# A decoder layer's attention stage: nine threshold searches dealt gap by gap, and the sixteen query blocks in another order

## The reference

```python
s = jnp.einsum('bqhd,bsd->bqhs', iqb, ikf)                       # 8 index heads of 64
idx_score = jnp.einsum('bqhs,bqh->bqs', jax.nn.relu(s), iwb * w_scale)
idx_score = jnp.where(causal[None], idx_score, NEG_INF)
_, sel = lax.top_k(idx_score, n_sel)                             # n_sel = 256
...
logits = jnp.where(valid[:, :, None, None, :], logits, NEG_INF)
p = jax.nn.softmax(logits, axis=-1)
```

## Time and profile before

| | us |
|---|---|
| median of 3 runs | 4710.19 |
| lowest and highest | 4708.51, 4710.79 |
| the profiled execution | 4710.05 |
| its span in the trace | 4708.1 |
| attention in it, first logits to the end of the last block's values | 613.8 to 1898.7 |

### The profile page before, as it was taken

The page is one execution under the profiler, slowest core; times in us unless marked ns, Lnnn a source line. Parts: engine busy times, 40 slices in busy tenths (PEclk is TensorE's granted clock), DMA queues, the critical chain, the costliest instruction groups (busy, mean ns, idle before and its releaser), DMA issues. The chain is left out here.

```text
span 4708.1 us, 69036 instructions
## 1 busy us (share of the span) xinstructions
PE 4350.5 (92%) x24163; PEld 3164.7 (67%) x24163; DVE 3098.5 (66%) x4884; ACT 1816.1 (39%) x2677; POOL 933.7 (20%) x1126
## 2 busy tenths in 40 slices
PE   8999978899988887399999999999999999999987
PEld 4444434444444443299998988989899998998961
DVE  2567747887778885245555655657566776776767
ACT  1222233343433333133334444444444555555530
POOL 0000012121111112211111212212122222222235
PEclk9999989999999998699999999999999999999996
DMA  5444230011010000344445536455466566666668
GB/s 187 119 121 123 66 93 24 21 25 19 15 28 15 15 13 14 97 148 165 156 136 208 191 138 228 170 200 201 174 224 217 208 231 229 213 232 225 217 219 335
DMA packets 525084, 666.35 MB, mean 142 GB/s; under 512 B 59201, under 2 KB 389441, under 8 KB 524897
## 3 DMA queue, kind: packets, MB, share of 16 engines
q1 hardware_dynamic: 400368, 484.87, 31.1%
q10 hardware_dynamic: 97984, 93.93, 6.1%
q0 software_dynamic: 26576, 85.56, 4.7%
HBM read 543.93 MB, written 120.36 MB: 141 GB/s over the span
## 5 line engine op out<-in xcount | busy, mean ns | idle before, releaser
L1956 DVE TENSOR_TENSOR w_lo<-w_raw,w_hi 128x2048 fp32r<-128x2048 f32 x386 | 874.5, 2286 | 557.7 <-ACT w_hi L2040 557.7
L1864 PE MATMUL gu<-x_hi,w_hi 128*128 128x240 f32 (+8 forms) x4096 | 1196.1, 292 | 21.5 <-DVE up L1971 15.7
L1867 PE MATMUL gu<-x_lo,w_hi 128*128 128x240 f32 (+8 forms) x4096 | 1192.6, 291 | 0.0
L1868 PE MATMUL gu<-x_hi,w_lo 128*128 128x240 f32 (+8 forms) x4096 | 1190.9, 291 | 0.0
L2040 ACT ACTIVATE w_hi<-w_raw 128x2048 fp32r<-128x2048 f32 x386 | 726.2, 1905 | 260.8 <-issue 144.5
L1864 PEld LDWEIGHTS gu<-x_hi,w_hi 128*128 128x128 f32 x4096 | 771.9, 188 | 25.8 <-DVE up L1971 18.9
L1868 PEld LDWEIGHTS gu<-x_hi,w_lo 128*128 128x128 f32 x4096 | 772.6, 189 | 0.0
L1867 PEld LDWEIGHTS gu<-x_lo,w_hi 128*128 128x128 f32 x4096 | 772.4, 189 | 0.2
L1838 POOL TENSOR_TENSOR a_lo<-up,a_hi 128x384 fp32r<-128x384 f32 x256 | 396.6, 1549 | 1213.6 <-ACT a_hi L2052 1213.6
L533 PE MATMUL proj_acc<-w_in_sb,hT 128*128 128x512 f32 (+1 forms) x1280 | 495.9, 535 | 0.7 <-ACT hT L549 0.7
L1864 PE MATMUL yp<-w_hi,a_hi 128*128 128x512 f32 x1088 | 445.4, 409 | 2.7
(11 more groups left out here) (299 smaller groups left out, 5734.4 us busy)
## 6 DMA issues: line engine op xcount, KB each, us to landing
w_raw<-w_gate_up SPq DMA_DIRECT2D x258, 1024.0 KB, 7.1
w_raw<-w_down SPq DMA_DIRECT2D x128, 1024.0 KB, 6.8
y_dram<-y_rows ACTq DMA_DIRECT2D x128, 256.0 KB, 2.2
y_dram<-zeros ACTq DMA_DIRECT2D x12, 2688.0 KB, 14.6
h_blk<-h_dram SPq DMA_DIRECT2D x32, 512.0 KB, 8.4
y_dram<-y_rows ACTq DMA_DIRECT2D x128, 128.0 KB, 6.5
qi_dram<-qi_stage ACTq DMA_DIRECT2D x16, 640.0 KB, 3.2
x_in<-x SPq DMA_DIRECT2D x16, 512.0 KB, 6.2
```

The costliest lines, as they stand in the source:

```text
L1864: op = nc.tensor.matmul(out, s_hi_, m_hi, start=(n == 0), stop=False)
L1867: nc.tensor.matmul(out, s_hi_, m_lo, start=False, stop=False)
L1868: op = nc.tensor.matmul(out, s_lo_, m_hi, start=False, stop=(n == len(pairs) - 1))
L1956: nc.vector.tensor_tensor(w_lo[:, c % 2, cols], raw[:, c % 3, cols], w_hi[:, c % 2, cols].bitcast(F32), ALU.subtract).then_inc(s_lo, 1)
```

## The change

`PHASES` and its dealing are gone. `ORDER` is written by hand, and a function `plan` walks through the 96 gaps once, with an estimated clock for TensorE and one for VectorE. It gives hosted pieces to a gap whenever a search may be scored, and passes of the current search to a gap as long as the estimated VectorE ends no later than a little after the next logits. When a block's own search is not done by the time it is needed, all that is left of it goes into the gap ahead. `select` counts as a 33rd pass and may stand in any gap. In the first three steps a slot takes two hosted pieces, not one. The order of masks loaded from DRAM follows the new order of blocks.

```diff
-    PHASES = ((0, 1, 2), (3, 7), (4, 15), (5, 14), (6, 13), (12,), (11,), (10,), (9,), (8,))
+    ORDER = (0, 1, 7, 3, 6, 14, 15, 4, 11, 12, 5, 10, 13, 9, 2, 8)
...
+        for n, (k, i) in enumerate(gaps):
+            b = ORDER[k]
+            if i == 0 and b >= EARLY:
+                own = SEARCHED.index(b)
+                if s <= own:
+                    assert s == own and scored[s] < n - 1
+                    vector += sum(cost(s, x) for x in range(bit, BITS + 1))
+                    take(gaps[n - 1], s, bit, BITS + 1)
...
+            if host < N_SEARCH and (host < 2 or chosen.get(host - 2, n) < n and chosen_at[host - 2] <= tensor + 2000):
+                for place in (slot for slot in some for _ in range(2 if k < 3 else 1)):
+                    if step < STEPS * halves[host]:
+                        hosted.setdefault(place, []).append((host, step))
+                        step += 1
+                        fill += 650
...
+            while s < N_SEARCH and scored.get(s, n) < n and (s < 2 or free.get(SEARCHED[s - 2], n) < n):
+                if not bit:
+                    vector = max(vector, done)
+                if vector + cost(s, bit) * 0.6 > tensor + logits:
+                    break
+                vector += cost(s, bit)
+                take((k, i), s, bit, bit + 1)
...
-            select(k)
...
-                    if users and keys[k] <= EARLY * P // 2:
-                        users = [j for j in users if j % 2 == k % 2]
+                    users = [j for j in range(k) if loaded[j] and (
+                        max(keys[j], keys[k]) > EARLY * P // 2 or j % 2 == k % 2)]
```

More of the change, by code:

```diff
@@ L655, in attend_stage @@
     UNITS = ((0, 0), (1, 1), (2, 0), (3, 1), (1, 0), (0, 1), (3, 0), (2, 1))
-    PHASES = ((0, 1, 2), (3, 7), (4, 15), (5, 14), (6, 13), (12,), (11,), (10,), (9,), (8,))
-    SEARCHED = tuple(b for blocks in PHASES for b in blocks if b >= EARLY)
+    ORDER = (0, 1, 7, 3, 6, 14, 15, 4, 11, 12, 5, 10, 13, 9, 2, 8)
+    SEARCHED = tuple(b for b in ORDER if b >= EARLY)
     assert SEARCHED[0] == EARLY
-    ORDER = tuple(b for blocks in PHASES for b in blocks)
-    PHASE = tuple(p for p, blocks in enumerate(PHASES) for b in blocks)
     N_SEARCH = len(SEARCHED)
@@ L670, in attend_stage @@
     cut = [(b + 2) // 2 for b in ORDER]
[L672 to L692, removed]
     def values_part(k, g, part):
@@ L697, in values_part @@
         return range(cut[k]) if part == 0 else range(cut[k], ORDER[k] + 1)
[L699 to L726, removed]
@@ L728, in attend_stage, with places, plan, cost @@
-    upto = bits()
+    def places(k, i):
+        if i == 0:
+            return [("values", k - 1, 1, c) for c in range(ORDER[k - 1] + 1)] if k else []
+        if i < 3:
+            return [("half", k - 1, i - 1, c) for c in range(4)] if k else []
+        if i < 5:
+            return [("values", k, 0, c) for c in values_part(k, 0, i - 3)]
+        return [("tail", k, 0, c) for c in range(4)] if k < 3 else []
+    def plan():
+        hosted, last_of, bits = {}, {}, {}
+        gaps = [(k, i) for k in range(TILES) for i in range(HEADS)]
+        scored, chosen, chosen_at, free = {0: -1}, {}, {}, {}
+        host, step, s, bit = 1, 0, 0, 0
+        tensor, vector = 20000.0, 0.0
+        def cost(s, n):
+            return s_keys[s] * 1.045 + 870 if n < BITS else s_keys[s] * 6.0 + 2500
+        def take(gap, s, first, last):
+            entries = bits.setdefault(gap, [])
+            if entries and entries[-1][0] == s:
+                entries[-1][2] = last
+            else:
+                entries.append([s, first, last])
+        for n, (k, i) in enumerate(gaps):
[6 more added lines that the diff above has]
+                    take(gaps[n - 1], s, bit, BITS + 1)
+                    chosen[s], chosen_at[s] = n - 1, vector
+                    s, bit = s + 1, 0
+                tensor = max(tensor, chosen_at[own])
+            logits = keys[k] * 2.2 + 300
+            done = tensor + logits
+            some = places(k, i)
+            fill = (300, 7700, 7700, 0, 800, 5000)[i] * (k > 0 or i > 2) + 1000 * len(some) * (i in (0, 3, 4))
+            if host < N_SEARCH and (host < 2 or chosen.get(host - 2, n) < n and chosen_at[host - 2] <= tensor + 2000):
[4 more added lines that the diff above has]
+                        fill += 650
+                        if step == STEPS * halves[host]:
+                            name, of, g, c = place
+                            part = c >= cut[of] if (name, g) == ("values", 0) else 0
+                            last_of[name, of, g, part] = host
+                            scored[host] = n
+                if host in scored:
+                    host, step = host + 1, 0
+            vector = max(vector, done) + keys[k] * 1.06 + 350
+            exp = vector + keys[k] * 0.72 + 750
+            vector += (3000, 0, 0, 6000, 0, 300)[i]
+            tensor = done + fill
+            if not halved(k) and i == 4:
+                tensor = max(tensor, vector + keys[k] * 0.72 + 450)
+            elif not halved(k) or i == 4:
+                tensor = max(tensor, exp)
+            if i in (0, 3) and fill > 2000:
+                tensor = max(tensor, exp + fill - 3000)
+            if i == HEADS - 1:
+                free[b] = n
+            while s < N_SEARCH and scored.get(s, n) < n and (s < 2 or free.get(SEARCHED[s - 2], n) < n):
[5 more added lines that the diff above has]
+                take((k, i), s, bit, bit + 1)
+                bit += 1
+                if bit > BITS:
+                    chosen[s], chosen_at[s] = n, vector
+                    s, bit = s + 1, 0
+        assert host == s == N_SEARCH
+        return hosted, last_of, bits
@@ L730, in walk, with halved @@
+    def halved(k):
+        return keys[k] <= SEQ // 2
+    hosted, last_of, bits = plan()
     def walk(do):
@@ L749, in search @@
         def search(k, i):
[L750 to L757, removed]
+            if "search" in do:
+                for s, first, last in bits.get((k, i), ()):
+                    do["search"](s, first, min(last, BITS))
+                    if last > BITS:
+                        do["select"](s)
         for k in range(TILES + 2):
@@ L1014, in fetch, with apart @@
                     sp.dma_start(h[:], D_["h"][b * P:(b + 1) * P, :]).then_inc(s_hl, 16)
+                def apart(k):
+                    return not loaded[k] or max(keys[k], keys[k + 1]) <= EARLY * P // 2
                 def logits(k, i):
@@ L1019, in logits @@
                             load_q(k + 1)
-                            if loaded[k + 1] and (not loaded[k] or keys[k + 1] <= EARLY * P // 2):
+                            if loaded[k + 1] and apart(k):
                                 load_mask(k + 1)
@@ L1027, in late @@
                 def late(k):
-                    if k + 1 < TILES and loaded[k + 1] and loaded[k] and keys[k + 1] > EARLY * P // 2:
+                    if 0 < k and k + 1 < TILES and loaded[k + 1] and not apart(k):
                         load_mask(k + 1)
```

3 lines of the change are left out of this document (removed).

## The result

| | before | after |
|---|---|---|
| median, us | 4709.35 | 4742.59 |
| lowest to highest | 4702.45 to 4710.79 | 4741.64 to 4744.75 |
| ratio, 95% interval | | 1.0074 (1.0057 to 1.0092) |
| profiled span | 4708.1 | 4742.8 |

The change makes the kernel 33 us slower. 4751 was forecast, and the time lies inside the range of 4723 to 4778.

A forecast was written before the change was run, and what follows sets the result against it. TensorE and VectorE were both taken as near their limit in the attention stage, so only TensorE's idle time would change: 50 - 29 + 20 = +41 us on 4710.05 gave 4751, range 4723 to 4778.

The forecast's parts named there:

- the six waits: Sign: TensorE's waits for VectorE's mask grow from 63 us in 5 times to over 110 in 6.
- the longest before block 15: Sign: TensorE's longest mask wait is about 36 us; gap 5 of step 5 lasts about 45 us.
- step 2: Sign: block 7's step lasts 90 to 95 us with 16 us waiting for ReLU; under 82 would mean pairs are free.
- Term 1: Gap 5 of steps 1, 5, 8, 11, 12, 14: rest of each search paid there, idle 125.9 us against 75.5, +50.
- Term 2: Selects beside other work, in steps 4, 7, 10, and lighter steps 13, 14: idle 16 us against 45.3, -29.
- Term 3: Pairs of hosted pieces: 37 more at 0.8 us TensorE idle each, less overlaps and one input wait; +20, bounds 0 and +30.
- The mask loads: Attention stage: 4.9 us of waiting moves to block 6's mask at step 4, sum unchanged, bounds -4 and +3.
- TensorE's clock: Attention stage: effect of longer waits on the granted clock left out at 0, bounds -3 and +3 us.
- my two marks: TensorE's stage busy time: within 10 us of 1112 if right, moved by over 15 us if wrong.
- thin idle time: Some 37 us of TensorE idle time spread over the rest of the attention stage; no change in the forecast sum.
- the even dealing wins: Rival: row maxima never late outside the six gaps, stage 14 us shorter, 4696; decides at 47 us idle there; chance 0.07.

The follow-up runs named there:

- e3: Changed kernel with the 8 passes of block 15's search in gap 5 of step 5 left out: 4716.82 us.
- e6: Changed kernel with two plan numbers raised, a chunk of values 1000 to 1100 ns and a hosted piece 650 to 900: 4696.86 us, ratio 0.998 to the kernel before.
- e5: Changed kernel with block 6's late mask load issued after the logits of gap 5, ahead of the h1 store and h fetch: 4737.39 us.
- e7: e6 plus VectorE allowed 0.8 of a pass past the next logits (was 0.4), two-piece slots in steps 0 and 1 only, and e5's edit: 4660.59 us.
- e8: e7 with another order of blocks (0, 3, 4, 7, 2, ...) and two pieces to a slot in step 0 only: 4624.18 us, ratio 0.982 to before.
- e2: Changed kernel with the old order of blocks under the new plan: 4765.55 us, ratio 1.0126 to the kernel before.
- e4: Kernel before, with every hosting slot taking two pieces and the next none, 128 pairs for 3: 4767.52 us, ratio 1.0127.

## Why the prediction was right, and where it was off

**The place and the mechanism** were right: the steps and gaps, the six waits (126.4 us, "over 110"), the longest before block 15 ("about 36", 35.9 measured), and step 2 at 93.7 us ("90 to 95") with 14.0 us of waits for ReLU and score copies. e3 and e6 confirm the cause. The size, 8 us from the forecast, is in part luck, as the sum at the end shows.

**Term 1** (+50) measured +55. The six gaps were forecast at 32.5, 44.9, 25.3, 36.9, 29.1 and 10.6 us and last 32.7, 45.1, 25.8, 37.4, 29.5 and 11.7. Five of them were forecast to within 0.5 us from durations in the old trace, and the last to within 1.1; in these gaps VectorE works almost alone. The lengths are 2.9 over in sum. The rest of the 5 is TensorE's work in them, 51.6 for 53.4: with 8 hosted pieces gap 5 of step 1 has 10.4, where I took 12.5.

**Term 2** (-29) measured -25: steps 4, 7, 10, 13 and 14 have 6.0, 3.7, 2.2, 2.3 and 6.4 us beside gap 5, 20.6 for the 16 that I had left them. Behind the `select` in gap 2 of step 4 TensorE waits 4.5, where I took 3.

**Term 3** (+20) measured +18: TensorE waits 30.2 us for ReLU and score copies, where it waited 5.3 before, and the wait of 6.7 for the fetch of h is gone.

**The mask loads** were a step that failed. I moved 4.9 us and set bounds of -4 and +3; the waits grew by 8.3, from 8.7 to 17.0. The 4.9 us are the wait for the first mask of the stage, and that stays (5.2 now). The late load is the other one: 3.8 us before, at the end of step 2, and 11.8 now, at the end of step 3. It takes longer there. The DMA view (out<-in, queue, size, median us from issue to landing) of the kernel before in 745 to 753 us, and then of the changed kernel in 875 to 888 us:

```profile
GB/s 20 31 0 0 0 0 0 0 0 164 205 82 143 348 410 369 369 430 241 394 476 369 399 430 323 50 32 16 0 0 0 0 3 0 0 0 0 0 3 0
...
h_blk<-h_dram SPq DMA_DIRECT2D x1, 512.0 KB, 3.3
q_blk<-qi_dram SPq DMA_DIRECT2D x1, 384.0 KB, 4.1
mask_early<-mask_dram SPq DMA_DIRECT2D x1, 128.0 KB, 3.3
```

```profile
GB/s 0 0 0 77 25 0 0 0 0 176 76 126 151 76 63 88 139 113 63 50 50 63 31 103 91 122 99 70 76 106 104 100 115 76 222 321 340 199 19 0
...
h_blk<-h_dram SPq DMA_DIRECT2D x1, 512.0 KB, 10.6
q_blk<-qi_dram SPq DMA_DIRECT2D x1, 384.0 KB, 11.7
mask_early<-mask_dram SPq DMA_DIRECT2D x1, 224.0 KB, 11.3
```

All three loads take about three times as long, and the bytes move at some 100 GB/s in place of 350 to 430. The mask of the changed kernel is larger, but `h_blk` has the same 512 KB in both. What differs in the trace is the order in time: the four token scatters of GpSimd start at 870.49 to 874.43 us there, ahead of these loads (875.29 to 876.18), and in the kernel before they start at 746.99 to 751.10, behind the loads. In e5 the mask load is issued at 870.88, ahead of the scatters, and TensorE has no wait for it at 875.61, while the `q_blk` load behind the scatters still takes 12.4 us.

The trace of the kernel before already had slow loads behind scatters, and TensorE waited for none of them. These are from its window 1136 to 1149 us:

```profile
h_blk<-h_dram SPq DMA_DIRECT2D x1, 512.0 KB, 10.4
...
mask_early<-mask_dram SPq DMA_DIRECT2D x1, 224.0 KB, 11.3
```

After step 1 the kernel before fetches `h_blk` 12 times behind all four scatters of a step, and it lands after 6.8 to 10.4 us; the three fetches with none or one of the four ahead of them take 3.3 to 3.7. In the changed kernel the fetches behind all four take 4.6 to 11.4, and the one with none ahead 3.5. So the scatters are the likely cause, but I ran no kernel without them, and it stays argued. I had looked at which load is late, and had priced its landing by the fast ones.

**TensorE's clock** was the other step that failed. Busy time was to stay within 10 us of 1112 and fell by 12.4, between my two marks. I had left the clock at nothing with bounds of 3 us either way; it is worth 11 (last section).

**The sum.** In idle time, 55.1 - 24.7 + 18.2 + 8.3 is 56.9. The stage's idle time grew by 47.1, so some 10 us of thin idle time went, probably because the plan has fewer late maxima. The fall in busy time then takes it to +34.6, for the +41 that I had. So the errors cancel in part: the terms and the mask loads together were 16 us too low, the thin idle time and the busy time 22 us too high, and those last two stood at nothing in the sum.

The rival "the even dealing wins" had the point of decision right: 47 us of idle time outside the six gaps. The changed kernel has 89. e7 and e8 have more than 47 there too (110 and 88 beside their mask waits); they are faster than before because hardly any mask wait is left.

## What to carry to other kernels

When work is dealt from one engine's queue into another's gaps under a deadline, what isn't dealt in time is paid in full at the deadline, while a little too much dealt costs only some late pieces (36.8 us of waits against 108.7 in e7): so let the plan's estimate of the host engine err on the long side, and look first for forced remainders in what the plan deals. Price such a remainder from the old trace as the sum of the instructions in it; that was good to 2%. Judge an order and a dealing together: each alone was slower here by 49 and 59 us, the two with better numbers (and the edits of e7) were 47 us faster than before, and another order with such numbers 83.

## What the runs showed of the hardware

TensorE's busy time moved by 23 us between kernels with the same matmuls. I laid the granted clock of the trace over the busy stretches of the stage, counted each microsecond at 1.2 GHz as half, and counted the stretches at 1.2 GHz:

| kernel | stage | idle | busy | of it at 1.2 GHz | as if at 2.4 GHz | stretches at 1.2 GHz | waits over 3 us |
|---|---|---|---|---|---|---|---|
| before | 1284.9 | 172.7 | 1112.2 | 98.3 | 1063.1 | 22 | 13 |
| changed | 1319.6 | 219.8 | 1099.8 | 75.6 | 1062.0 | 15 | 11 |
| e2 | 1333.4 | 241.1 | 1092.3 | 63.8 | 1060.4 | 14 | 11 |
| e4 | 1343.2 | 228.0 | 1115.1 | 108.3 | 1061.0 | 21 | 11 |
| e7 | 1239.4 | 127.9 | 1111.6 | 102.1 | 1060.5 | 20 | 9 |
| e8 | 1198.5 | 103.4 | 1095.1 | 72.4 | 1058.9 | 12 | 7 |

The column "as if at 2.4 GHz" is the same to 0.4%, so the work is the same, and what differs is the time spent on it at the lower level. (The ends of matmuls are modelled in these traces, so this is as good as the model.) It doesn't follow the idle time: the kernel before has less idle time than the changed kernel and more work at 1.2 GHz. It goes by the number of stretches at the low clock: each holds 4.5 to 6.0 us of TensorE's work on average. That doesn't go by the length of the wait: the stretch that begins in the wait of 35.9 us holds 5.3 us of work, and that of the 9.6 us wait in the earlier trace rows 5.2. After either, the first two matmuls take 2.05 us. Nor is a long wait needed: each kernel has more such stretches than waits over 3 us, e4 21 for 11. One begins at 969.6 us in the kernel before, where no wait nearby is over 1.9 us.

The Trainium skill (TensorE: Matmul & The Clock Gate, "HAM oscillation — how this bites in real kernels") counts this cost once for each idle stretch in its example; the six long waits of the changed kernel agree with that, with one low stretch for each and 3.1 to 5.3 us of work in it. By the table the change had a gain of 11 us that I didn't forecast, a quarter of what its idle time cost.

A load of 512 KB took 10.6 us to land right behind four small scatters, for 3.3 us ahead of them. GpSimd, too, waited 11.29 us for those scatters in e5.
